# DeltaNet's block substitution on two engines, Hyena's first spectral block with the taps, and four reorderings, in a one-layer hybrid mixer and mixture-of-experts kernel

## Time and profile before

| What | Value |
|---|---|
| Time, median of 3 runs | 1939.4 us (1939.26 to 1940.89) |
| The profiled execution's own time | 1937.27 us |
| Its span, first to last instruction | 1935.4 us |
| Granted TensorE clock, mean | 0.929 of full speed |
| TensorE busy (matmul) | 87% of the span |
| VectorE, ScalarE, GpSimd busy | 57%, 45%, 20% |

### The profile page before, as it was taken

One profiled execution on the slowest core, in us unless ns is written; L12 is line 12 of the kernel. 1 busy time (PEld: TensorE's weight loads), 2 busy tenths in 40 slices (PEclk: granted clock), 3 DMA queues, 4 the chain that ended last, 5 costly groups with the idle time before them and its releaser, 6 DMA issues. The chain is left out here.

```text
span 1935.4 us, 20344 instructions
## 1 busy us (share of the span) xinstructions
PE 1678.7 (87%) x7711; PEld 1199.6 (62%) x7711; DVE 1109.0 (57%) x1220; ACT 875.7 (45%) x1202; POOL 390.3 (20%) x468
## 2 busy tenths in 40 slices
PE   6799999987997499998898889816999999999981
PEld 2453755474556489744356657715888888888861
DVE  3640643176354456653323433377889888888873
ACT  4130343253336366522000034424777777777752
POOL 0000410081005785000213415401010010100101
PEclk9989999988998799999898999957999999999986
DMA  9730200040007533300420233136999999999966
GB/s 374 240 135 1 88 1 0 1 174 0 1 2 221 165 89 90 119 26 14 148 105 0 87 143 122 64 141 233 392 395 386 402 381 400 395 383 398 381 228 195
DMA packets 109623, 344.64 MB, mean 178 GB/s; under 512 B 36135, under 2 KB 45994, under 8 KB 84822
## 3 DMA queue, kind: packets, MB, share of 16 engines
q1 hardware_dynamic: 100220, 318.56, 43.6%
q0 software_dynamic: 5328, 18.88, 4.0%
q10 hardware_dynamic: 3977, 5.90, 1.1%
HBM read 308.07 MB, written 35.23 MB: 177 GB/s over the span
## 5 line engine op out<-in xcount | busy, mean ns | idle before, releaser
L3020 DVE TENSOR_TENSOR w_lo<-w_raw,w_hi 128x2048 fp32r<-128x2048 f32 x192 | 438.4, 2291 | 65.6 <-ACT w_hi L2962 65.6
L2962 ACT ACTIVATE w_hi<-w_raw 128x2048 fp32r<-128x2048 f32 x192 | 368.0, 1917 | 145.0 <-PE ps L2912 134.5
L549 PE MATMUL ps<-hT,w_mixer 128*128 128x512 f32 (+1 forms) x768 | 310.7, 564 | 5.3 <-PEq L187 3.6
L549 PEld LDWEIGHTS ps<-hT,w_mixer 128*128 128x128 f32 x768 | 146.3, 193 | 158.5 <-issue 155.2
L2910 PE MATMUL ps<-w_hi,xsT_hi 128*128 128x512 f32 x512 | 203.0, 396 | 2.4 <-DVE xsT_lo L3025 2.4
L2912 PE MATMUL ps<-w_hi,xsT_lo 128*128 128x512 f32 x512 | 200.4, 391 | 0.0
L2911 PE MATMUL ps<-w_lo,xsT_hi 128*128 128x512 f32 x512 | 200.1, 391 | 0.0
L2878 POOL DMA_INDIRECT moe_sum<-y,idx_col x15 | 30.3, 2017 | 461.2 <-ACT y L2982 430.2
L2910 PEld LDWEIGHTS ps<-w_hi,xsT_hi 128*128 128x128 f32 x512 | 96.8, 189 | 22.0 <-DVE xsT_lo L3025 2.8
L2912 PEld LDWEIGHTS ps<-w_hi,xsT_lo 128*128 128x128 f32 x512 | 96.5, 189 | 20.5
L2911 PEld LDWEIGHTS ps<-w_lo,xsT_hi 128*128 128x128 f32 x512 | 96.7, 189 | 19.4
(11 more groups left out here) (482 smaller groups left out, 2969.7 us busy)
## 6 DMA issues: line engine op xcount, KB each, us to landing
w_raw<-in_moe_w_gate SPq DMA_DIRECT2D x64, 1024.0 KB, 7.0
w_raw<-in_moe_w_up SPq DMA_DIRECT2D x64, 1024.0 KB, 8.8
w_raw<-in_moe_w_down SPq DMA_DIRECT2D x64, 1024.0 KB, 9.1
w_mod_row<-in_w_mod SPq DMA_DIRECT2D x32, 512.0 KB, 4.8
w_mod<-in_w_mod SPq DMA_DIRECT2D x8, 1024.0 KB, 14.3
w_mixer<-in_w_in SPq DMA_DIRECT2D x4, 2048.0 KB, 11.5
dn_ma<-dn_ma SPq DMA_DIRECT2D x16, 512.0 KB, 3.5
dn_mT<-dn_ma SPq DMA_DIRECT2D x20, 256.0 KB, 3.5
```

The source lines that it names most:

```text
L549: last = nc.tensor.matmul(S.ps[:, 3 * (i % 2) + c, 0:n], S.w[:, k, b["col"]:b["col"] + P], S.hT[:, k, t0:t0 + n], start=(x == 0), stop=(x ...
L2962: nc.scalar.activation(wh[q % RING][:, :], S.raw[q % RAW][:, :], ACT.Copy).then_inc(s.hi, 1)
L3020: nc.vector.tensor_tensor(wl[q % RING][:, :], S.raw[q % RAW][:, :], wh[q % RING][:, :].bitcast(F32), ALU.subtract).then_inc(s.lo, 1)
```

## The change

1. hT is scaled at the start of gla_p in place of the end of the modulation stage, the latents first. TensorE's first group waits for each column group, in the order 3, 0, 4, 1, 5, 6, 2, 7; group q = 2 waits for the context.
2. In project_conv the norm's part comes ahead of the side's start, on ScalarE and VectorE.
3. GpSimd does the first 20 of the 31 steps of group 0, VectorE the last 11, after its own work of that stage. The eight block loads are issued by SyncE (direction 0) and ScalarE (direction 1).
4. hy_f makes the first spectral block too: after tap tile n, TensorE multiplies tile n - 2. The taps use two pairs of PSUM banks in place of three. hy_k is left with blocks 1 to 3, and its table loads come a block earlier.
5. The inverse transforms of hy_d run over b on the outside: order 0 in two groups of four results, order 1 with all four results at once.
6. In project_out's last tile VectorE does both additions that GpSimd does in the others.

```diff
@@ modulate: removed from the end of its ScalarE and VectorE programs
-            for st, c0, c1 in ((1, 0, CTX), (0, CTX, TOK)):
-                for k in range(KS):
-                    nc.scalar.activation(S.hT[:, k, c0:c1], S.hT[:, k, c0:c1], ACT.Identity,
-                                         bias=S.mod1[:, 1, st, k:k + 1], scale=S.mod1[:, 0, st, k:k + 1])
...
@@ project_conv
+            norm.act(s, act)
             side.start_act(s, act)
-            norm.act(s, act)
...
+            norm.dve(s, dve, ch)
             side.start_dve(s, dve, ch)
-            norm.dve(s, dve, ch)
@@ gla_p, TensorE
+                    if q == 2:
+                        pe.wait_ge(s.scaled_a, 2 * SCALED)
+                        pe.wait_ge(s.scaled_v, 2 * (KD - SCALED))
+                    order = (3, 0, 4, 1, 5, 6, 2, 7) if q == 0 else range(KD)
+                    for x, k in enumerate(order):
+                        if q == 0 and k < SCALED:
+                            pe.wait_ge(s.scaled_a, k + 1)
+                        if q == 0 and k >= SCALED:
+                            pe.wait_ge(s.scaled_v, k - SCALED + 1)
@@ gla_p, VectorE, ahead of all else (ScalarE alike, k in range(SCALED), SCALED = 3)
+            for st, c0, c1 in ((0, CTX, TOK), (1, 0, CTX)):
+                for k in range(SCALED, KD):
+                    nc.vector.tensor_scalar(S.hT[:, k, c0:c1], S.hT[:, k, c0:c1], S.mod1[:, 0, st, k:k + 1],
+                                            S.mod1[:, 1, st, k:k + 1], ALU.mult, ALU.add).then_inc(s.scaled_v, 1)
@@ dn_a: SyncE, ScalarE, GpSimd, VectorE (HANDED = 20)
-            sp.wait_ge(s.sub, 1)
+            sp.wait_ge(s.sub, 2)
             put_blocks(sp, 0, s.d_st)
             sp.wait_ge(s.d_st, 16)
-            for d in range(2):
-                load_blocks(sp, 0, d)
+            load_blocks(sp, 0, 0)
...
+            act.wait_ge(s.zeroed, 1)
+            act.wait_ge(s.d_st, 16)
+            load_blocks(nc.scalar, 0, 1)
...
-            substitute(nc.gpsimd, pc).then_inc(s.sub, 1)
+            substitute(nc.gpsimd, pc, 0, HANDED).then_inc(s.sub, 1)
...
+            dve.wait_ge(s.sub, 1)
+            substitute(nc.vector, Chain(dve, s.chain), HANDED).then_inc(s.sub, 1)
@@ hy_f, TensorE
+            for n in range(LT + 2):
+                if n < LT:
+                    if n >= 2:
+                        pe.wait_ge(s.tapped, n - 1)
...
+                if n >= 2:
+                    lt = n - 2
+                    if lt == 0:
+                        pe.wait_ge(s.tables[0], 2 * 16)
+                    for q, (x, done) in enumerate(((hs, s.sums), (hd, s.diffs))):
+                        pe.wait_ge(done, lt + 1)
+                        last = nc.tensor.matmul(S.ps[:, 2 * q + lt // HT, :], tw[0][:, q, lt, :],
+                                                x[:, lt, :, :].rearrange("p o c -> p (o c)"),
+                                                start=(lt % HT == 0), stop=(lt % HT == HT - 1))
+            last.then_inc(s.first, 1)
+            pe.wait_ge(s.first, 1)
@@ hy_k, TensorE
-            for b in range(HT):
+            for b in range(1, HT):
@@ hy_d, TensorE, order 0, then order 1
-                    for nt in range(LT):
-                        if nt >= 2:
-                            pe.wait_ge(s.z, nt - 1)
+                    for g in range(2):
                         for b in range(HT):
-                            if nt == 0:
+                            if g == 0:
                                 pe.wait_ge(s.y, b + 1)
+                            for nt in range(4 * g, 4 * g + 4):
+                                if g == 1 and b == 0:
+                                    pe.wait_ge(s.z, nt - 3)
...
-                    for i in range(4):
-                        par, c = i // 2, i % 2
-                        for b in range(HT):
-                            if i == 0:
-                                pe.wait_ge(s.y, HT + b + 1)
+                    for b in range(HT):
+                        pe.wait_ge(s.y, HT + b + 1)
+                        for i in range(4):
+                            par, c = i // 2, i % 2
@@ project_out, VectorE (GpSimd breaks off its loop at t == LT - 1)
+                    if t == LT - 1:
+                        dve.wait_ge(s.y_sc, LT)
+                        dve.wait_ge(s.x_in[t % 2], 16 * (t // 2 + 1))
+                        nc.vector.tensor_tensor(x1[:, t, :], tm[t % 2][:, :], xt[t % 2][:, :], ALU.add).then_inc(s.x1d, 1)
...
+                    if t == LT - 1:
+                        dve.wait_ge(s.h2m, LT)
+                        nc.vector.tensor_tensor(h2[t % 2][:, :], h2[t % 2][:, :], rows[:, 2, :], ALU.add).then_inc(s.h2d, 1)
```

More of the change, by code:

```diff
@@ L176 @@
 ADDED = 4
+SCALED = 3
+HANDED = 20
 SPENT = []
@@ L367, in _ @@
             dve.wait_ge(s.evac_v, T)
-            for st, c0, c1 in ((1, 0, CTX), (0, CTX, TOK)):
-                for k in range(KS, KD):
-                    nc.vector.tensor_scalar(S.hT[:, k, c0:c1], S.hT[:, k, c0:c1], S.mod1[:, 0, st, k:k + 1],
-                                            S.mod1[:, 1, st, k:k + 1], ALU.mult, ALU.add)
         @s.block.tensor
@@ L857, in _ @@
         def _(act):
+            for st, c0, c1 in ((0, CTX, TOK), (1, 0, CTX)):
+                for k in range(SCALED):
+                    nc.scalar.activation(S.hT[:, k, c0:c1], S.hT[:, k, c0:c1], ACT.Identity,
+                                         bias=S.mod1[:, 1, st, k:k + 1], scale=S.mod1[:, 0, st, k:k + 1]
+                                         ).then_inc(s.scaled_a, 1)
             for i, (col, m, dst, scale) in enumerate(cms):
@@ L1496, in take_blocks, with substitute @@
         return ops.tensor_copy(bl[0:64, :, :], bu[0:64, :, :].rearrange("q r c -> q c r"))
-    def substitute(ops, ch):
-        for j in range(DB - 1):
+    def substitute(ops, ch, first=0, end=DB - 1):
+        for j in range(first, end):
             i, c = DB - 1 - j, j + 1
@@ L1505, in substitute @@
             last = ops.tensor_tensor(bd[:, j + 1:DB, 0:c], bd[:, j + 1:DB, 0:c], t, ALU.subtract)
-            if j < DB - 2:
+            if j < end - 1:
                 ch(last)
@@ L2347, in hyena @@
     fwd_in = nc.alloc_semaphore("hy_fwd_in")
-    with Stage(nc, "hy_f", "tables taps tapped zeroed sums diffs") as s:
+    with Stage(nc, "hy_f", "tables*2 taps tapped zeroed sums diffs first") as s:
         plan.at = mark + LT * DG * 4
@@ L2361, in _ @@
                                  A["dft_whole"][q, :, b * P:(b + 1) * P].rearrange("(t p) k -> p t k", p=P)
[L2362 removed]
+                                 ).then_inc(s.tables[b], 16)
             for q in range(2):
                 sp.dma_start(fwd[:, q, :, :], A["dft_fwd"][q].rearrange("(t p) k -> p t k", p=P)).then_inc(fwd_in, 16)
[L2365 removed]
+            sp.wait_ge(s.tables[1], 2 * 16)
         @s.block.tensor
         def _(pe):
[L2369 to L2376 removed]
+            for n in range(LT + 2):
+                if n < LT:
+                    if n >= 2:
+                        pe.wait_ge(s.tapped, n - 1)
+                    for q in range(2):
+                        r = slice(q * side.HF, (q + 1) * side.HF)
+                        last = nc.tensor.matmul(S.ps[:, 4 + 2 * (n % 2) + q, :], h[r, n * P:(n + 1) * P], w4[r, :],
+                                                start=True, stop=True)
+                    last.then_inc(s.taps, 1)
+                if n >= 2:
[9 more added lines that the diff above has]
+            pe.wait_ge(s.first, 1)
         @s.block.vector
@@ L2380, in _ @@
             for lt in range(LT):
-                x, bank = tap[lt % 2], 2 + 2 * (lt % 3)
+                x, bank = tap[lt % 2], 4 + 2 * (lt % 2)
                 if lt == 0:
```

45 lines of the change are left out of this document (21 added, 24 removed).

## The result

| | Before | After |
|---|---|---|
| Median, us | 1939.3 (1938.8 to 1940.9, 4 runs) | 1894.5 (1890.2 to 1898.0, 4 runs) |
| Profiled execution, its own time and its span | 1937.3, 1935.4 | 1890.2, 1888.4 |
| Granted clock, mean | 0.929 | 0.941 |

The ratio is 0.9767, with a 95% interval of 0.9746 to 0.9787. Five further runs of the same kernel gave 1892.4 (1890.4 to 1897.1) and again 0.9767 (0.9752 to 0.9782). The forecast of 1892.3 with a range of 1889 to 1898 held. Between the two profiled executions 47.0 us are gained, where the sum said 47.1.

The account below looks back on a forecast made before the run. TensorE, busy in 87% of the span, bounds most stages; its waits are what is left. Terms 3.4 + 7.3 + 5.3 + 9.5 + 19.3 + 2.3 = 47.1 us take 1937.3 to 1890.2, plus 2.1 for the median: 1892.3, range 1889 to 1898.

Parts of the forecast that it names:

- the held value: Start of gla_p: GpSimd's 1.16 us memset holds VectorE's first scaling, so TensorE gains 3.4 us; free, 4.3.
- the rule that was cited with it: In gla_p: a two-port tensor_scalar and a GpSimd instruction exclude each other for the whole instruction.
- ScalarE's slack: In dn_c: ScalarE's delayed work has block 0's convolution at about 481, TensorE wants it at 482.8; covered by 1.8 us.
- the clause against the first rival: Sign of a wrong forecast: clock rows at 0.50 inside L2519, L2530 or hy_f after the table's landing.
- the first rival: Clock falls to 1.2 GHz in hy_d's rotated inverse transforms, costing 55 us; 1947 us in all; chance 3%.
- The spectral products: Rival in hy_f: they starve, TensorE runs at 1.2 GHz between taps, block 1 is 8 later; 1910 us; chance 5%.
- ScalarE and the store: Rival: ScalarE late in dn_c and store late in dn_a, eating 4 of part 2 and 3 of part 3; 1899; 7%.
- Order 1's gain: Rival in hy_d: this gain is absent because VectorE and GpSimd fall behind TensorE's closer products; 1902 us; chance 3%.

Follow-up runs that it names:

- undo_scaling: Changed kernel with hT scaled at the end of the modulation stage again, context first, and TensorE's waits for the scalings removed; 1896.4 us (one run).
- memset_late: Changed kernel with GpSimd's memset of gla_lrT waiting until VectorE has scaled all its column groups; median 1894.4 us.
- undo_first_block: Changed kernel with hy_f and hy_k put back to those of the kernel before; median 1906.5 us (1906.4 to 1910.8).
- fill_order0: Changed kernel with order 0 of hy_d keeping all eight results open in eight PSUM banks; median 1891.2 us, ratio 0.9758.

## Why the prediction was right, point by point

**Part 1, forecast 3.4, measured 3.3** (undo_scaling). The choice of the held value was right, and memset_late shows the reason: 0.86 us. What this says of the rule that was cited with it (the Trainium skill, SBUF — State Buffer, Who interferes with whom): this case's trace agrees in kind and not quite in size: the memset went on for 1.11 us after VectorE had begun (to 56.90), and the scaling was 0.85 longer than without it, so it was not held for all of that time. The page of the profile says itself that GpSimd's spans are rough. TensorE started at 57.60 and not at 57.15: the modulation ended 0.3 later than assumed, the barrier took 0.63 where 0.25 was assumed, TensorE followed the scaling by 0.15, and the held scaling took 1.66 where 1.96 was assumed. Between the two kernels' traces the start moved by 2.95.

**Part 2, forecast 7.3, measured 7.7** between the two kernels and 7.6 undone. ScalarE's slack behind it was forecast as 1.8 and is 1.8.

**Part 3, forecast 5.3, measured 6.0** at the transposes. VectorE's 22 operations were put at 7.6 and took 7.56. Two small terms were off. VectorE started right behind GpSimd (0.04 us), where the sum had 0.4. And the sum had the transposes start 4.0 us behind the first load's issue, for the loads' landing; they start 3.8 us after it, 1.5 behind the barrier, which is what VectorE's own memsets need; nothing waits for a landing there, only TensorE's first product does (657.04, "DMA dn_diag").

**Part 4, forecast 9.5, measured 9.15**, and 9.3 undone. The sum said 10.0, and 9.5 was taken in case the clock fell, which it didn't. Two terms were off in opposite directions. The second table landed 5.75 us after the start and not 7.0. In exchange a tile takes 2.97 us and not 2.67: between tap tiles a product takes 0.96 where 0.86 was taken from the long row of 16, and the tap tile 1.06 where 0.95 was taken, all at a granted clock of 1.00. Going back and forth between banks is not the reason: the last products of hy_f do that too, without tap tiles between them, and are 0.86 apart. What in the mixture costs the 0.1 is open.

**Part 5, forecast 19.3, measured 19.97**, just above the 19.6 that was given as its bound. Order 0 gave 9.5 (forecast 9.8), with the one wait left at 1.94 (forecast 2.0); order 1 gave 9.4 from the forward transform's start (forecast 9.5), and 10.2 when it was undone, where the 52 instructions behind the long wait took 25.41 in place of 24.62. The remaining 1.0 is the first forward transform, 30.59 before and 29.55 after: the clock at the stage's start. The forecast didn't have it, part 5 doesn't cause it, and whether part 4 does is open (undo_first_block).

**Part 6, forecast 2.3, measured 2.4 on the last tile, 1.3 on the stage.** The 2.4 is from the start of VectorE's first scaling of the tile to the end of the last addition (before 1254.69 to 1263.90, after 1210.01 to 1216.85). But the stage is shorter by only 1.3: the tile's scaling comes 0.7 later after the stage's start (118.71 against 118.03; 117.9 to 119.3 in all traces of the new kernels), and between the last router step and the experts' first transposes it takes 0.4 more (10.69 against 10.31; 10.4 to 10.8). No run undoes part 6, so whether these are its doing is open.

**The rivals.** The clock stayed at 1.00 in the rotated inverse transforms of the changed kernel (L2561's 64 instructions in 27.63, 0.43 each), so the clause against the first rival held. In two other traces it fell behind order 0's one wait and cost 1.7 us, which part 5 had named as possible. The spectral products did not starve. ScalarE and the store were not late. Order 1's gain is there.

**What was luck.** By stages the six parts gained 2.95, 7.74, 6.1, 9.15, 19.97 and 1.3 us, against 3.4, 7.3, 5.3, 9.5, 19.3 and 2.3; the other rows of the table lost 0.2 between the two traces. Errors of up to 1.0 in both directions cancel, and single stages differ by as much between two executions of one kernel. That the sum hit 47.0 to 0.1 is therefore in part luck; that each part is there, at about its size, is not.

**What was missed** is not a step but a spread. The forecast took the offset between a profiled execution and the median, 2.1 us, from the kernel before. The changed kernel's profiled execution lies 4.3 us below its median, so that 47.0 us gained in the rows became 44.8 in the medians. The profiled execution was also the fastest of its four. All nine runs of the changed kernel have their median at 1894.3.

## What to carry to other kernels

Where stages end in barriers, read the bounding engine's gaps one by one and cost each by the row that would take its place; six such terms came out within 1.0 us each of what their stages show (their sum within 0.1, partly by luck), and five of them were undone, whole or in pieces, and came back alone (the last tile was only read from its rows). Let the loop over a late operand be the outer one, with as many results open as there are banks: it turned waits of 9 and 7 us into one of 2, and in fill_order0 into none. Check a chain's gain on the whole stage as well: of the last tile's 2.4 us only 1.3 arrived. A part of 1 to 4 us is to be read from its stage's rows, because the medians of this kernel scatter by 8.

## What the runs showed of the hardware that was not expected

TensorE's clock at a stage's start is not fixed by the program. After the same gap of 3.56 us and the same instructions ahead of it, the first forward transform of hy_d took 29.55 us in ten traces and 27.86 in two; in the two with the old hy_k, the kernel before among them, it took 30.6. Timeline of TensorE in memset_late, then windows of its first 4 us and of the same 4 us in the changed kernel (29.55):

```profile
975.51 27.86 PE L2537 MATMUL ps<-hy_v,hy_fwd 128*128 128x256 f32 x128 [3.56 <-PEq L197]
```

```profile
975.50:979.50 4.00, 3.99 (x19) 3.54 (x20) 0.00 (x0) 0.00 (x0) 0.00 (x0) 1.00 0.73 217
```

```profile
971.20:975.20 4.00, 4.00 (x12) 3.24 (x13) 0.00 (x0) 0.00 (x0) 0.00 (x0) 0.62 0.69 212
```

Gaps of 1.7 us (mb_c, 5 of 13 traces) and 1.9 us (order 0, 2 of 10) cost another 1.5 to 1.7 us in some executions and nothing beyond their length in the rest. So a gap behind unbroken work had different prices here in executions of the same instructions, its length and up to 1.7 us besides (2.7 if the old hy_k is counted in), and closing it takes that scatter away as well. What decides between the two is open.
